# Stick-breaking attention on TensorE: steps taken two by two, both turns and scores first, then both applications

## The reference

```python
for q0 in range(0, seqlen, SB_QBLOCK):
    qb = q[:, q0:q1]; kb = k[:, :q1]; vb = v[:, :q1]
    z = jnp.einsum("bqhd,bkhd->bhqk", qb, kb) * scale
    strict = s_pos < t_pos
    log_keep = jnp.where(strict, jax.nn.log_sigmoid(-z), 0.0)
    after = lax.cumsum(log_keep, axis=3, reverse=True) - log_keep
    weights = jnp.where(strict, jnp.exp(jax.nn.log_sigmoid(z) + after), 0.0)
    outs.append(jnp.einsum("bhqk,bkhd->bqhd", weights, vb))
```

## Time and profile before

| quantity | value |
|---|---|
| median of three runs | 2596.04 us |
| profiled execution | 2595.95 us, span 2594.2 us |
| TensorE (PE) busy over the span | 2519.3 us, 97% |
| DVE, ACT, POOL busy | 64%, 52%, 61% |
| mean granted TensorE clock | 0.987 of full speed |
| chain that ended last, PE share by line | L2412 (output) 13%, L1968 (turn) 6%, L1983 (apply) 5%, L1950 (scores) 4% |

### The profile page before, as it was taken

The page is one execution under the profiler, slowest core; times in us unless marked ns, Lnnn a source line. Parts: engine busy times, 40 slices in busy tenths (PEclk is TensorE's granted clock), DMA queues, the critical chain, the costliest instruction groups (busy, mean ns, idle before and its releaser), DMA issues. The chain is left out here.

```text
span 2594.2 us, 40300 instructions
## 1 busy us (share of the span) xinstructions
PE 2519.3 (97%) x13783; PEld 1777.0 (68%) x13783; DVE 1673.0 (64%) x2074; ACT 1352.2 (52%) x2113; POOL 1578.4 (61%) x1391
## 2 busy tenths in 40 slices
PE   5999999998999999989999999999999999999998
PEld 3888777777888888866655555555555555688887
DVE  7332556546213565267788889898888989765553
ACT  5333333345333333344387888787788878522221
POOL 4676666687777777658876667676676767200000
PEclk8999999999999999989989999999999999999999
DMA  3543333333433333256741221312122121432330
GB/s 117 162 143 121 121 106 119 111 102 122 151 108 124 126 127 122 94 138 178 197 135 50 66 89 35 91 50 76 56 66 82 42 90 54 150 103 92 97 97 33
DMA packets 204101, 268.74 MB, mean 104 GB/s; under 512 B 13441, under 2 KB 137665, under 8 KB 197265
## 3 DMA queue, kind: packets, MB, share of 16 engines
q1 hardware_dynamic: 203632, 266.30, 32.3%
q10 hardware_dynamic: 288, 0.13, 0.0%
HBM read 169.36 MB, written 97.03 MB: 103 GB/s over the span
## 5 line engine op out<-in xcount | busy, mean ns | idle before, releaser
L2119 POOL TENSOR_TENSOR a_w<-a_beta,a_rest 128x1024 f32<-128x1024 f32 (+2 forms) x320 | 560.9, 1753 | 266.2 <-DVE a_rest L2067 149.0
L804 POOL TENSOR_TENSOR f_l_lo<-f_wst,f_l_hi 128x512 fp32r<-128x512 f32 x312 | 408.0, 1311 | 293.6 <-ACT f_l_hi L667 293.3
L2067 DVE TENSOR_TENSOR_SCAN a_rest<-a_keep,a_rest,a_floor 128x513 f32<-128x513 f32 x384 | 468.4, 1260 | 10.8 <-ACT a_keep L2021 10.8
L1968 PE MATMUL a_turn<-a_ident,a_w 128*128 128x128 f32 (+1 forms) x2432 | 347.6, 281 | 9.2 <-DVE a_wt L2005 6.3
L1968 PEld LDWEIGHTS a_turn<-a_ident,a_w 128*128 128x128 f32 (+1 forms) x2432 | 256.1, 139 | 118.3 <-issue 92.3
L533 PE MATMUL f_xz<-f_t_hi,f_l_hi 128*128 128x512 f32 x832 | 328.6, 395 | 0.0
L533 PE MATMUL f_xz<-f_t_hi,f_l_lo 128*128 128x512 f32 x832 | 325.0, 391 | 0.0
L533 PE MATMUL f_xz<-f_t_lo,f_l_hi 128*128 128x512 f32 x832 | 324.8, 390 | 0.0
L2005 ACT COPY a_wt<-a_turn 128x512 f32<-128x512 f32 (+3 forms) x456 | 233.3, 531 | 169.2 <-PE a_turn L1968 167.7
L2021 ACT ACTIVATE a_keep<-a_z 128x1024 f32<-128x1024 f32 (+4 forms) x352 | 300.3, 853 | 3.3 <-PE a_z L1950 3.2
L2021 ACT ACTIVATE a_beta<-a_z 128x1024 f32<-128x1024 f32 (+4 forms) x352 | 300.1, 853 | 1.5 <-POOL a_w L2133 1.3
(11 more groups left out here) (300 smaller groups left out, 4372.4 us busy)
## 6 DMA issues: line engine op xcount, KB each, us to landing
f_wst<-in_w_pairs SPq DMA_DIRECT2D x52, 1024.0 KB, 5.9
scratch_gate<-outs SPq DMA_DIRECT2D x64, 256.0 KB, 2.5
o_g<-scratch_mixed SPq DMA_DIRECT2D x32, 512.0 KB, 5.5
outs<-in_x SPq DMA_DIRECT2D x20, 512.0 KB, 4.6
scratch_xbc<-outs SPq DMA_DIRECT2D x36, 256.0 KB, 2.1
scratch_q_hi<-outs SPq DMA_DIRECT2D x32, 256.0 KB, 3.5
scratch_q_lo<-outs SPq DMA_DIRECT2D x32, 256.0 KB, 3.8
scratch_v<-outs SPq DMA_DIRECT2D x32, 256.0 KB, 2.3
```

The source lines that it names most:

```text
L804: return nc.gpsimd.tensor_tensor(out, a, b, op).then_inc(done, 1)
L1968: mm = nc.tensor.transpose(turn[h][0:rows, qi * P:(qi + 1) * P], tile[:, h, x:x + rows], ident[:, :])
L2067: mm = nc.vector.tensor_tensor_scan(rest[r % RS][:, h, tn - 1::-1], top, low, start, ALU.mult, ALU.max)
L2119: done = nc.gpsimd.tensor_tensor(tile[:, :, 0:tn], beta[r % KEEPS][:, :, 0:tn], rest[r % RS][:, :, 1:tn + 1], ALU.mult)
```

## The change

TensorE's loop now takes two values of n at a time. For both it issues the turn and the scores, and then for both the application. With m even, a pair of steps is T(m), S(m+9), T(m+1), S(m+10), A(m-1), A(m). No other engine's order changes, and no instruction is added or removed.

```diff
-            for n in range(-2, N + LAG + 1):
-                if 0 <= n - LAG < N:
-                    turn_block(n - LAG)
-                if 0 <= n - LAG - 1 < N:
-                    apply(n - LAG - 1)
-                if 0 <= n + 2 < N:
-                    scores(n + 2)
+            for first in range(-3, N + LAG + 2, 2):
+                for n in (first, first + 1):
+                    if 0 <= n - LAG < N:
+                        turn_block(n - LAG)
+                    if 0 <= n + 2 < N:
+                        scores(n + 2)
+                for n in (first, first + 1):
+                    if 0 <= n - LAG - 1 < N:
+                        apply(n - LAG - 1)
```

## The result

The changed kernel takes 2692.43 us, the median of six runs (2691.66 to 2699.19), against 2596.34 us for the one before: a ratio of 1.0375, interval 1.0365 to 1.0386, 96 us slower. The prediction was 2676 us, with a range of some 2640 to some 2715.

A forecast was written before the change was run, and what follows sets the result against it. PE's own order was taken to set the pace, other engines having slack. From 2595.95 us: minus 26 (passages), plus 83 (`beta` waits), plus 35 (gate multiply, DVE's queue), minus 12 (present idle time) gives 2676 us; range some 2640 to some 2715.

The forecast's parts named there:

- The gain: On PE, one passage between kinds of work fewer per pair: 0.15 us for each of 176 pairs, 26 us.
- ACT's chain: A pair's second scores wait for `beta` behind ACT's copies: 0.24 or 0.72 us in wide pairs, 83 us in all.
- (a): At units 13 and 43, DVE's gate multiply falls between two adjacent applications: 0.95 us each, 15 us in all.
- (b): Around unit 4, the gate multiply holds back DVE's scans and the copy of unit 6: that pair loses 1.9 us.
- (c): The same lateness of DVE's queue at m = 16 and m = 18: 0.4 and 0.2 us.
- What was taken back: Today's PE idle time that goes, as at unit 7 and two smaller DVE waits: 12 us, at least 7.
- a case of 19 in 100: Rival 'More': DVE a second bound, 2700 us, or more if pauses make the granted clock fall; chance 19%.
- 2656 us: Rival 'ACT's wait alone': PE's pauses let DVE catch up and its queue's lateness stays hidden; chance 25%.
- The faster rival: Second scores don't wait, `beta` being done within 2.93 us of the turn; only saved passages count, 2570 us; chance 4%.

The follow-up runs named there:

- odd_double: The changed kernel with the turns copied twice by ScalarE moved from m = 0, 4, 8, ... to 1, 5, 9, ...: 2675.38 us, ratio 1.0301.
- wide_only: The kernel before, paired only at units 10, 12, 24, 26, 32 and 34: 2611.83 us, ratio 1.0071.
- ends_apart: The changed kernel with the pairs that begin at units 0 and 14 done in the order of before: 2665.58 us, ratio 1.0267.
- ends_only: The kernel before, paired only at units 0 and 14, where chunks meet: 2621.52 us, ratio 1.0107.
- four_pairs: The kernel before, paired only at units 20, 22, 36 and 42: 2591.62 us, ratio 0.9984.
- other_parity: The changed kernel with pairs begun one step later, so that m is odd for a pair's first turn: 2689.97 us, ratio 1.0358.
- narrow_apart: The changed kernel with the pairs at units 4, 6 and 8 in the order of before: 2658.1 us, ratio 1.0245.

## Why the prediction was right

- **The gain.** Foreseen 26 us, measured 22. Where one of the two applications is of 128 queries, the saved passage is worth 0.01 us or less, so 18 of 22 pairs gain, not all. Why it is worth nothing there is not shown.
- **ACT's chain.** Foreseen waits of 0.24 and 0.72 us, measured 0.24 and 0.73; over all pairs 83 and 81 us. `odd_double` and `wide_only` show that the copies ahead of `beta` are the cause. One pair differs: at 18 the foreseen 0.64 us are 0.05, since PE has already waited 0.75 us for DVE's copy inside T(19). In `ends_apart`, where that copy is in time, they are 0.62.
- **(a) The gate multiply between two applications.** Foreseen 0.95 us each, measured 1.01 and 1.06 over both applications, also when alone in `ends_only`.
- **(b) and (c) DVE's queue.** DVE's timeline of the changed kernel around unit 4 shows the step as worked out:

```profile
1706.52 0.69 DVE L2078 TENSOR_TENSOR o_fw<-a_gate,a_o 128x512 f32<-128x512 f32 x1 [1.64 <-PE a_o L1983]
1707.13 2.45 DVE L2069 TENSOR_TENSOR_SCAN a_rest<-a_keep,a_rest,a_floor 128x513 f32<-128x513 f32 x2
1709.49 0.67 DVE L2007 COPY a_wt<-a_turn 128x512 f32<-128x512 f32 x1
```

  DVE waited for A(4), made the two scans, and then the copy that the second half of T(7) at 1710.21 waits for. The reader is to see that DVE was idle for 1.64 us and still late afterwards. T(7) costs 14 us in all, where 15 were foreseen; the wait at T(16) is 0.38 us for 0.4, but that at T(19) is 0.75 where the prediction had 0.2 for that pair. One reading behind this was off: three transposes of a half take 0.38 us undisturbed and not 0.33, so the wait at unit 7 before was 0.79 us and not 0.84.
- **What was taken back.** Foreseen 12 us, measured some 14 of waits of the kernel before that are no more or stand in the new sums.
- **The term that was missing** is half clock, 16 us in this execution, with 3 us of query waits. The forecast gave it as part of a case of 19 in 100 and put nothing in the sum. It said that the clock had stayed at 1.00 with single waits of 0.8 us. In head pair 3 there are now, at A(0), S(12), S(14), T(7) and S(18), five pauses of 0.7 to 1.8 us within 24 us. The six runs differ by 7.5 us where those of before differ by 1.5, and the longest has the lowest mean clock (0.981 against 0.983 to 0.985), so it is likely this term that varies from run to run. Another 4 us are the gain that was put too high, and 4 us the copy at T(19) that was put too low.
- **The range.** Its lower end does not follow from its words: 2656 us with a gain of 51 in place of 26 is 2631, not some 2640. The measured time is far from that end.
- **The faster rival** asked for the chain to be under 2.93 us. It was 3.17 (T(14) at 1733.17 to the scores at 1736.34), and only pairs where `beta` is narrow behave as it says: `four_pairs` takes four of them. The trace agrees there with the rule of the Trainium skill (TensorEngine Tiling (Array Packing), Key Properties) that a change of tiling mode drains TensorE: two applications in a row save 0.15 us. In the sum that gain is outweighed.

## What to carry to other kernels

When work of the busiest engine is reordered, ask for each wait in the new order what stands ahead of its releaser in the *other* engine's queue, and measure both ways from one common event. Here the engine that set the pace gave up 1.01 us of cover to save 0.15. The other engines had been idle for 12 to 30% of the stage, and that did not help: each takes its work in the written order, so what stands behind a late product is late too. A saving by order may still be had in places where the partner's work is short, so apply it by place and not by rule. Where one queue is paired and its partner is changed to match, walk the partner's loop too.

## What the hardware showed

- The passage between kinds of TensorE work costs 0.15 us where both applications are of 256 queries or more, and almost nothing (0.01 us) with an application of 128 queries.
- The clock fell to its lower level behind waits that lie close together, and not by their size alone. With S(14), T(7) and S(18) waiting 0.47, 1.61 and 1.27 us (`ends_apart`) it fell in one head pair of eight, 3 us in the stage. With a gate wait of 1.01 us ahead of them, and queries that are late in some head pairs (the change), it fell in six, 34 us; in `other_parity` 68 us. With the waits at T(7) and S(18) cut to 0.33 us or nothing (`narrow_apart`) it never fell. What else decides, as between head pairs 2 and 7 of the change, is not shown.
- In the unchanged order, waits on PE repeat from head pair to head pair: 0.78 to 0.79 us at T(7), 0.29 to 0.30 at T(19), 0.29 to 0.33 at T(36), with 0.82 there in the last one.
